# A running inverse kept in the other partition half, in the chunks of a recurrent mixer

## The reference, cut to what matters

```
def rwkv7_scan(r, w, k, v, a_vec, b_vec):
    # S_t = S_{t-1} diag(w_t) + (S_{t-1} a_t) b_t^T + v_t k_t^T ; y_t = S_t r_t
    def step(s, inp):
        r_t, w_t, k_t, v_t, a_t, b_t = inp
        sa = einsum('bhvk,bhk->bhv', s, a_t)
        s = s * w_t[:, :, None, :] + sa[..., None] * b_t[:, :, None, :] + v_t[..., None] * k_t[:, :, None, :]
        return s, einsum('bhvk,bhk->bhv', s, r_t)
...
mean, var = mean and variance of y over each head
y = (y - mean) * rsqrt(var + GN_EPS) * ln_x_w + ln_x_b
y = y + sum(r_h * k_h * r_k, per head) * v_h
return y * g
```

## Time and profile before

| | us |
|---|---|
| runs | 2386.71, 2387.95, 2388.24 |
| median | 2387.95 |
| profiled execution, device time | 2388.29 |
| its span | 2386.5 |
| of the span: first projections | 0 to 193 |
| the five chunks of the recurrence | 193 to 501 |
| everything behind them | 501 to 2386.5 |

### The profile page before, as it was taken

How to read it: one execution, slowest core, us unless ns; L and a number is a source line. 1 busy time by engine, 2 the same in 40 slices (tenths; PEclk the granted TensorE clock), 3 DMA queues, 4 the chain that set the end, 5 groups by cost and what they waited for, 6 DMA issues and landing times.

```text
span 2386.5 us, 51839 instructions
## 1 busy us (share of the span) xinstructions
PE 2360.2 (99%) x20636; PEld 2212.0 (93%) x20636; DVE 1538.0 (64%) x1958; ACT 1070.5 (45%) x1366; POOL 124.2 (5%) x156
## 2 busy tenths in 40 slices
PE   9999999999999999999999999999999999999997
PEld 9998999999999999999889999899888888888897
DVE  7586775665865656565444677648877777774444
ACT  5543333345534434444444446555444444444442
POOL 2000000001200000000000110012000000000000
PEclk9999999999999999999999999999999999999999
DMA  7443233345555555555555474355555555555553
GB/s 259 156 159 116 90 100 100 108 153 169 185 183 183 181 184 176 187 182 185 188 190 185 150 253 138 117 176 172 181 192 177 193 192 177 193 189 190 187 182 125
DMA packets 116958, 406.01 MB, mean 170 GB/s; under 512 B 12848, under 2 KB 19984, under 8 KB 116560
## 3 DMA queue, kind: packets, MB, share of 16 engines
q1 hardware_dynamic: 111936, 396.07, 51.4%
q10 hardware_dynamic: 4880, 7.82, 1.0%
HBM read 401.69 MB, written 2.15 MB: 169 GB/s over the span
## 4 chain that ended last, share of the span: by engine, by line
PE 94%; DVE 3%; ACT 1%; issue 1%; POOL 0%; DMA 0%; DVEq 0%; ACTq 0%; POOLq 0%
PE ps L1712 23%; PE ps L1714 12%; PE ps L1716 11%; PE ps L1718 11%; PE ps L1717 11%; PE ps L1892 3%; PE ps L1881 3%; PE ps L1688 2%; PE ps L1689 2%; PE ps L1690 2%; PE ps L1882 2%; PE ps L1883 2%; PE ps L1900 2%; PE ps L2201 1%; PE ps L2203 1%; PE ps L2202 1%
## 5 line engine op out<-in xcount | busy, mean ns | idle before, releaser
L946 DVE TENSOR_TENSOR wl<-raw,wh 128x1024 fp32r<-128x1024 f32 x744 | 912.3, 1238 | 698.6 <-ACT wh L541 698.4
L541 ACT ACTIVATE wh<-raw 128x1024 fp32r<-128x1024 f32 x744 | 777.8, 1057 | 954.0 <-PE ps L1718 361.5
L1716 PE MATMUL ps<-xh,wh 128*128 128x256 f32 (+2 forms) x2048 | 582.4, 284 | 3.8 <-DVE wl L946 2.3
L1718 PE MATMUL ps<-xh,wl 128*128 128x256 f32 (+2 forms) x2048 | 580.5, 283 | 0.0
L1717 PE MATMUL ps<-xl,wh 128*128 128x256 f32 (+2 forms) x2048 | 580.1, 283 | 0.0
L1712 PE MATMUL ps<-x,wh 128*128 128x512 f32 x1280 | 448.2, 393 | 0.8 <-DVE wl L946 0.8
L1716 PEld LDWEIGHTS ps<-xh,wh 128*128 128x128 f32 x2048 | 387.1, 189 | 6.7 <-issue 3.6
L1717 PEld LDWEIGHTS ps<-xl,wh 128*128 128x128 f32 x2048 | 387.2, 189 | 0.2
L1718 PEld LDWEIGHTS ps<-xh,wl 128*128 128x128 f32 x2048 | 386.7, 189 | 0.0
L1712 PE MATMUL ps<-act,wh 128*128 128x512 f32 x1056 | 369.7, 393 | 0.0
L1714 PE MATMUL ps<-x,wl 128*128 128x256 f32 x1280 | 357.1, 279 | 0.0
(11 more groups left out here) (302 smaller groups left out, 3150.9 us busy)
## 6 DMA issues: line engine op xcount, KB each, us to landing
raw<-in_gate_up SPq DMA_DIRECT2D x176, 512.0 KB, 3.5
raw<-in_down SPq DMA_DIRECT2D x176, 512.0 KB, 4.2
raw<-in_up SPq DMA_DIRECT2D x176, 512.0 KB, 4.2
raw<-in_w_in SPq DMA_DIRECT2D x104, 512.0 KB, 3.5
raw<-in_in SPq DMA_DIRECT2D x48, 512.0 KB, 3.5
raw<-in_w_out SPq DMA_DIRECT2D x32, 512.0 KB, 3.6
raw<-in_out SPq DMA_DIRECT2D x32, 512.0 KB, 3.5
bias<-bias_rows ACTq DMA_DIRECT2D x1, 4096.0 KB, 25.7
```

The source lines that it names most:

```text
L541: act.activation(wh[:, slot], raw[:, slot], ACT.Copy).then_inc(high_ready, 1)
L946: dve.tensor_tensor(wl[:, slot], raw[:, slot], wh[:, slot].bitcast(F32), ALU.subtract).then_inc(low_ready, 1)
L1716: pe.matmul(out, w_high, hi, start=(k == 0), stop=False)
L1718: last = pe.matmul(out, w_low, hi, start=False, stop=(k == 2 * per - 1))
```

## The change

The products of P are written crossed, so `qb` and `tn` now lie in the other half from `tt`; `tt` itself is made from a crossed copy of `am` in bank 6, which 16 more matmuls write in the turn phase (`matrix_turned`), and VectorE adds the identity to it there instead of behind the gram phase. That makes one product of each join straight and the other crossed, and the two are now issued in turns, tile by tile, into two banks. Both adds of VectorE wait for the end of the joint phase.

Other steps are paired the same way, a straight with a crossed one: values with keys `b` in turn; the bonus sums of the chunk before with P1; the transposes of `k`, which leave the turn phase, and the means with P2; the variances with P3; the part of the right-hand side from the chunk with P4, its part from the state with P5 and the last join; `out_state` with update; and `y` with the next state in output, in two halves with a wait on both (`out_half`, `state_half`) between them. The bonus products of VectorE move to P1, ScalarE's exponentials for the next chunk (`decays`) from level 2 to level 1, its copy of `kt` to level 2, that of `zb` to the last level, and `inverse_spread(c - 1, 0)` behind the split of J3.

In the first chunk the fill behind gram grows from 2 halves to 3 and that behind turn shrinks from 2 to 1; the split of one weight chunk moves from ahead of `z_read(6)` to the end of VectorE's gram phase.

```diff
+FIRST_HALVES = {**HALVES, "gram": 3, "turn": 1}
...
-            lows(55, 5, 3)
+            lows(55, 4, 3)
             z_read(6)
...
-                dve.wait_ge(am_ready, level(c, 0))
-                dve.tensor_tensor(tt[:], am[0][:], over(identc[:], RT), ALU.add).then_inc(tt_ready, 1)
                 dve.wait_ge(dve_step, ga_step)
                 level_matrix(c, 1)
+                if c == 0:
+                    lows(59, 1, 3)
...
                 dve.tensor_tensor(tn[:], bank(7), over(identc[:], RT), ALU.add).then_inc(tn_ready, 1)
+                dve.tensor_tensor(tt[:], bank(6), over(identc[:], RT), ALU.add).then_inc(tt_ready, 1)
...
+                def matrix_turned():
...
+                    for f in range(RT):
+                        head(7, f, am[0][:, f], identc)
+                        last = head(6, f, identc, am[0][:, f], True)
+                    last.then_inc(am_turned, 1)
...
+                    def product(f):
+                        return head(4, f, am[l % 2][:, f], tn[:, f], True)
...
+                    elif l == 3:
+                        if c:
+                            pe.wait_ge(ysq_ready, c)
+                        for f in range(RT):
+                            last = product(f)
+                            if c:
+                                s_last = spread_of(7, c - 1, f)
+                        last.then_inc(q_done, 1)
...
+                    for f in range(RT):
+                        last = head(6, f, qb[:, f], tt[:, f])
+                        if not final:
+                            n_last = head(5, f, tt[:, f], qb[:, f], True)
+                        elif c and f < 4:
+                            z_last = z_state(f)
+                    last.then_inc(dt_done, 1)
...
+                for f in range(4):
+                    o_last = out_update(f)
+                    if c < LAST:
+                        s_last = state_update(4 + f)
+                o_last.then_inc(out_half, 1)
+                if c < LAST:
+                    s_last.then_inc(state_half, 1)
+                pe.wait_ge(out_half, c + 1)
+                if c < LAST:
+                    pe.wait_ge(state_half, c + 1)
+                for f in range(4):
+                    out_keys(f)
+                    if c < LAST:
+                        state_keys(4 + f)
```

More of the change, by code:

```diff
@@ L389, in program @@
         LAST = N_RC - 1
+        Z_BANK = [7] * LAST + [5]
         TA = T0[LAST - 1]
@@ L1902, in head, with head_sum, center_of, spread_of @@
                 return last
[L1904 to L1934, removed]
+            def head_sum(b, f, c, lhs, rhs):
+                for rows in HEAD_ROWS:
+                    last = pe.matmul(ps[rows, b, C * f:C * f + CHUNK_LENGTHS[c]], lhs[rows, rows], rhs[rows], start=True, stop=True)
+                return last
+            def center_of(b, c, f):
+                return head_sum(b, f, c, center, kn[:, f, T0[c]:T0[c] + CHUNK_LENGTHS[c]])
+            def spread_of(b, c, f):
+                return head_sum(b, f, c, bones, ysq[c][:, f, 0:CHUNK_LENGTHS[c]])
+            def bonus_of(b, c, f):
+                return head_sum(b, f, c, bones, z[:, 12 + f, 1 + T0[c]:1 + T0[c] + CHUNK_LENGTHS[c]])
             def gates(half):
@@ L1996, in _ @@
[L1996 to L2000, removed]
-                pe.wait_ge(am_ready, level(c, 0))
+                    return head(4, f, z[:, 20 + f, 1 + t0:1 + t0 + n], identc, f < 4, rows=n)
+                def matrix_turned():
+                    pe.wait_ge(k_masked, c + 1)
+                    pe.wait_ge(am_ready, level(c, 0))
+                    for f in range(RT):
+                        head(7, f, am[0][:, f], identc)
+                        last = head(6, f, identc, am[0][:, f], True)
+                    last.then_inc(am_turned, 1)
@@ L2016, in _, with z_chunk @@
                     last.then_inc(b_turned, 1)
-                pe.wait_ge(v_half, c + 1)
-                for f in range(4):
-                    last = turn_v(f)
-                last.then_inc(vb_turned, 1)
                 finish(c, "turn")
                 for l in range(1, LEVELS[c]):
+                    final = l == LEVELS[c] - 1
+                    def product(f):
+                        return head(4, f, am[l % 2][:, f], tn[:, f], True)
+                    def z_chunk(f):
+                        return head(Z_BANK[c], f, gak[:, f], vb[:, f], start=(f == 0), stop=(c == 0 and f == RT - 1))
@@ L2058, in _ @@
+                last.then_inc(u_done, 1)
                 finish(c, "update")
+                for f in range(4):
+                    out_keys(4 + f, c == 0 and f == 0)
+                    if c < LAST:
+                        state_keys(f)
                 pe.wait_ge(u_ready, c + 1)
-                def out_state(b, f, start):
-                    return head(b, f, st[:, f], now[:, f, 1, 0:n], start=start, stop=False, n=n)
-                def out_chunk(b, f, part, start=False, closing=False):
-                    lhs, rhs = ((vb, grk), (ub, grb))[part]
-                    return head(b, f, lhs[:, f], rhs[:, f, 0:n], f >= 4, start=start, stop=closing or (f == RT - 1 and part == 1), n=n)
@@ L2116, in _ @@
+                for f in range(4):
+                    o_last = out_update(4 + f)
+                    if c < LAST:
+                        s_last = state_update(f)
+                o_last.then_inc(y_done, 1)
+                if c < LAST:
+                    s_last.then_inc(s_done, 1)
                 finish(c, "output")
-            centers(LAST)
+            pe.wait_ge(y_ready, N_RC)
+            for f in range(RT):
+                last = center_of(7, LAST, f)
+            last.then_inc(centered, 1)
@@ L2119, in _ @@
             fill(SLOT[LAST, "center"])
-            spreads(LAST)
+            pe.wait_ge(ysq_ready, N_RC)
+            for f in range(RT):
+                last = spread_of(7, LAST, f)
+            last.then_inc(spread_done, 1)
             fill(SLOT[LAST, "var"])
```

253 lines of the change are left out of this document (129 added, 124 removed).

## The result

The changed kernel takes **2352.56 us** (median of four runs, 2352.25 to 2354.89), the kernel before 2388.09 beside it (2386.71 to 2389.79): ratio **0.9851**, 95% interval 0.9839 to 0.9863. That is 35.5 us less, where 39.1 were forecast; 2352.56 lies in the range of 2341 to 2358 and 3.8 above the point. So the mechanism held and the size was off by a tenth.

The account below looks back on a forecast made before the run. TensorE, busy 99% of the span, was taken to bound the kernel. Phases -39.4, chunk 0's waits -5.7 and new late waits +6.0 summed to -39.1 us, from 2387.95 to 2348.8; range 2341 to 2358.

Parts of the forecast that it names:

- The price of a pair in turns: TensorE's small matmuls: straight and crossed in turns cost 29 ns each, 0.93 us for two lots; all phases -39.4 us.
- The rival by which pairs would not overlap: Small matmuls outside gram would all cost 58.3 ns, making the kernel slower at 2397 us; chance 0.04.
- Chunk 0's waits: TensorE's waits for z_read(6) and z_shift(6) go and the clock stays full behind them: -5.7 us together.
- Chunk 1's wait for `tn`: P5 in chunk 1 waits 1.5 us for VectorE's add; with 0.1 at update, +1.6.
- chunk 0's read: P5's fill in chunk 0 already awaits a group read for 0.9 us, which comes later by +0.6.
- chunk 2's: Fill of P1 in chunk 2 awaits a group read that the shorter P1 no longer covers: +0.45 us.
- chunk 3's: Group read at J4 in chunk 3, with a reciprocal and a split in front of it: +0.9 us.
- the sentence on GpSimd: GpSimd's next keys also wait for turned k, some 20 us before gram needs them; nothing TensorE awaits is queued behind.
- ScalarE has room: ScalarE is busy 111 of 312 us around the chunks, so nothing TensorE awaits is queued behind its moved work.
- the drain: Wait between output's halves: +0.25 us for each of five and for chunk 0's turn_half, +1.5; bounds 0 and 0.5 each.
- J2 with P3 in the last chunk: Priced at 3.4 us, -0.5; separately, P3's wait for the add into tn adds +0.75.
- The variance of the last chunk: At the end the variance awaits a gate product that came 1.2 us ahead, while TensorE gains some 5: +0.5.

Follow-up runs that it names:

- pool_spread: Changed kernel with GpSimd's two bk sums set apart, the first waiting only for transposed b, the second also for transposed k; 2354.19 us, ratio 0.9858.
- keys_late: Changed kernel with chunk 1's VectorE key products, their reciprocals and unit_y(0) moved to the update phase; 2351.62 us, ratio 0.9844.
- three moves within VectorE's and TensorE's order: Changed kernel with chunk 1's key products later, chunk 0's second inverse_lengths behind P5's group read, last chunk's bonus products at its last join; 2348.38 us.
- straight_turns: Kernel before with each join's two products issued in turns into two banks, both straight, nothing crossed; 2390.3 us, ratio 1.0003.
- after_no_first: Changed kernel without the edits to the first chunk's border (fills 2 and 2, low split ahead of z_read(6)); 2359.39 us, ratio 0.9877.
- before_first: Kernel before with only the first chunk's border edits (fills of 3 and 1 halves, moved low split); 2384.42 us, ratio 0.9977.

## Why the prediction was right, and where it missed

**The price of a pair in turns: right.** Forecast for J1 1.08, P2 1.55, output 2.0 to 2.3; measured 1.09, 1.56, 2.46, output being outside its range by its wait in the middle (below). Every P, J and update phase of two lots in turns without a wait took 1.08 or 1.09, the turn phases 2.02 and in the last chunk 2.20 (2.3 forecast), P2 1.56, its last-chunk form 1.49. The price of 29 ns was read off half a phase in the profile before, and it carried 39.4 of the sum. The rival by which pairs would not overlap is out. It drew on a rule of the Trainium skill ("TensorE: Matmul & The Clock Gate", Part 3, "The mechanism"), that a weight load overlaps only matmuls of another row group; the traces disagree here, since a straight and a crossed pair of the same row groups run at 29 ns a matmul and two straight ones at 58.

**Chunk 0's waits: right, a little large.** 5.7 forecast; 5.1 and 5.4 by the medians of the two runs that isolate the edits, 5.2 and 5.1 by their traces.

**Chunk 1's wait for `tn`: right** at 1.5 (1.52), and chunk 0's read at 0.9 + 0.6 (1.52), chunk 2's at 0.45 (0.4), chunk 3's at 0.9 (0.64, phase 1.79 for 1.09).

**Missed: the read of `hg` in chunk 1, 1.36.** I had left 0.1 for that chunk beside `tn`. The step that failed is the sentence on GpSimd, that nothing TensorE awaits is queued behind its new wait. The sums themselves moved forward, which the prediction did not follow. In the kernel before the first one waited for ScalarE's `pinv` and started at 282.62; the change makes ScalarE's exponentials one level earlier, and the sum starts at 267.14. So it moved from a stretch where VectorE then idled 1.26 to one where it never does, and VectorE loses 2.0 us there instead of 0.9. I looked at who waits for GpSimd, not at who runs beside it. In `pool_spread` the wait fell by 0.34 where VectorE lost 0.4 less, so without GpSimd beside it most of the 1.36 should go; that is argued from one such step, and no run had it so. In `keys_late` the stretch is emptier, and there it is GpSimd that stands still (its first sum 2.36, VectorE's split beside it 1.21), so that run removes both at once.

**Missed: the fill behind J3 in the last chunk, 1.51.** I priced J3 at 1.08; it lasts 2.66. Timeline of the changed kernel, ScalarE and then TensorE:

```profile
445.68 1.57 ACT L767 ACTIVATE gatew<-ps,vec 128x258 f32<-128x258 f32 x4
...
447.30 0.39 PE L1881 MATMUL ps<-ych,wh 128*128 128x258 f32 x1 [1.51 <-ACT gatew L767]
```

J3 used to be three lots long and covered ScalarE's read of the gates ahead of it. "ScalarE has room" was true of the average and said nothing of this place, the very thing for which I had examined chunk 2's group read. The same list of "what stood under the phase that becomes shorter" would have found it.

**Missed in size: the drain.** 0.25 forecast for the wait between the halves of output; the phase lasts 2.46 for 2.02, so 0.44 in four chunks, and 0.2 in the last, which forms no next state. Chunk 0's turn has one too, with 0.17 for `z`: 2.73 for 2.27. Together +1.2. The upper bound of 0.5 held. No run took this wait out, so that the excess is its price is argued from the price of the matmuls.

**Smaller ones.** J2 with P3 in the last chunk lasts 4.54 for 4.15: TensorE stands 0.88 between the two; the add into `tn` that it needs starts at 437.69 and takes 0.69, and P3 starts at 438.48, so what the records put down as issue fits the add and its hand-over. The variance of the last chunk waits for nothing, where I had 0.5. Sum of the misses (`hg`, the fill behind J3, the output phases, chunk 0's turn, J2 with P3, the variance, chunk 3's read): 1.36 + 1.51 + 0.7 + 0.46 + 0.4 - 0.5 - 0.3 = 3.6, for 3.4 between 39.1 and 35.7. The three runs at 2352.3 to 2352.8, none of them profiled but by their distance those without the half clock, stand 3.1 to 3.6 above the 2349.2 forecast for the profiled one.

## What to carry to other kernels

Small matmuls of 64 by 64 use a quarter of the array each. A pair of them on the diagonal quadrants ran here beside a pair on the other two at no extra time, when both were issued in turns: look for one phase in the trace where that already happens, and price all others by it. When a phase gets shorter, list for each one what every other engine did under it, on the line and not in the mean: most of the waits that appeared are of that kind, and three moves within VectorE's and TensorE's order took away 4.7 of the 8.8 us. And when an instruction is let go earlier on GpSimd, look at what VectorE does at that moment, not only at who consumes the result.

## What the runs showed of the hardware that was not expected

- Two lots of 16, straight and crossed, one behind the other, overlap by 0.17 us at the border (1.84 for 2.01); two straight ones do not, one behind the other in the kernel before or in turns in `straight_turns` (2.01 both).
- A sum of GpSimd of 128x512, 1.2 to 1.3 us by itself, makes a VectorE instruction beside it 0.9 to 1.1 us longer: 0.29 becomes 1.41, 0.69 becomes 1.67, 1.22 becomes 2.22 (2.12 in the kernel before). In `keys_late` it is the sum that becomes 2.36.
- Where TensorE had stood still nowhere in the rows around it (541 to 558), but had gone over to matmuls of one column at 545.79, the clock stood at its lower level (0.50) for some 6 to 7 us in some profiles and for about half that in others, 2.1 to 2.4 and 0.6 to 0.8 us of time, and in four profiles not at all. In each it is the same place of the program.
- In chunk 0 of `after_no_first` the clock was full behind an idle piece of 1.76 us and at its lower level behind the next, of 2.07; in `before_first` it stayed full behind one of 0.6.
